# Weights fetched in order of use and cast by GpSimd, and the first block transposed on TensorE

## The chip, the cores and the metric

The kernel runs on the 8 cores of one Trainium2 chip, each core on 4 of the 32 sequences, with its own copy of the weights. No core talks to another. The metric is the device time of the slowest core in microseconds (us). Time before: 1548.24 us, the median of 3 runs (1544.91 to 1763.65).

## The reference

One layer of a streaming encoder, in float32:

```python
x = layer_norm(x, ln0_g, ln0_b)                      # entry norm, 1024 columns
proj = einsum('bsd,de->bse', x, w_in)                # w_in: 1024 x 4096
q, k, v, z_a, bg, cg, h, z_c = split(proj, 8)        # 512 columns each
# 8 heads of 64; a chunk of 64 frames sees itself and 8 chunks before it,
# with a learned relative bias
y_att  = chunk_attention(q, k, v, rel_bias) * silu(z_a)
y_conv = bg * causal_conv3(cg * h) * silu(z_c)
x = layer_norm(alpha * x + concat(y_att, y_conv) @ w_out, ln_g, ln_b)
```

The weights are 16.8 MB (`w_in`) and 4.2 MB (`w_out`) in float32; the kernel keeps both in SBUF in bf16. Each core has 4 x 2048 tokens.

## The kernel before

**Tiling.** The 8192 tokens of a core are 16 blocks of 512 tokens (`NTB`), each of 4 tiles of 128 tokens (`TPB`). A block goes through these stages: entry norm of its four tiles (`ln0_*`: statistics on DVE, four small GpSimd operations in `ln0_small`, two DVE passes over the tile in `ln0_res_a` and `ln0_res_b`, a bf16 copy `xhb` on ACT and a DMA transpose into `xnT` in `ln0_act`); `stage_P1`, 64 matmuls for q and k; `stage_attn`, eight heads, in which the score matmuls (`stage_QK`), the weighted sums of the head before (`stage_PV`) and the projections for v, z_a and the convolution (`unit_v`, `unit_za`, `unit_C`, `unit_zc`, `unit_B`, `unit_h`: 192 matmuls) are interleaved; then `stage_out`, 64 matmuls with `w_out`, and the last norm in `out_tile`. While block b is in `stage_attn`, the entry norm of block b+1 is done by DVE, GpSimd and ACT; `stage_P1(b+1)` runs before `stage_out(b)`. What `unit_h` leaves of the convolution for channel groups 2 and 3 (`late`) runs on DVE after the eight heads. Every fourth block (0, 4, 8, 12) begins a sequence and has no block before it to attend to.

**Order.** The program is written as one list per engine (`Prog`); each engine runs its list in order and waits on semaphores for what an instruction reads or overwrites. So the order in which the Python code calls `P.op` and `P.dma` is the order on each queue. All plain DMAs and DMA transposes are issued by SP (SyncE), in one queue. A GpSimd operation always waits for the one before it (`op`, line 62).

**Start of the kernel before.** SP issues the constant tables (lines 258 to 264: four 512 KB tables, three small ones, and `rtab` of 1 MB), then the four x tiles of block 0, then two weight chunks. All the tables count on one semaphore (`fix_dma_key`), so that the first DVE operation that reads any of them (line 275) waits for all. DVE scales the tables and builds `etab` (the bias, line 288) and then norms the four tiles. A weight chunk is 128 rows of `w_in` by 1024 columns, 512 KB (`wchunks`): the first eight chunks hold the columns of q and k, the next eight v and z_a, and so on. It lands in one of three staging buffers (`w_stage`: pieces of `yT`, `ytok`, later `xhb` and `xs`), and DVE casts it to bf16 (line 324). `w_item(n)` issues the DMA of chunk n+2 and casts chunk n. Chunks 0 to 15 stand ahead of `stage_attn(0)`; chunks 16 to 39 are background items (`bg`) of its heads 0, 1 and 2. The x tiles of block 1 are loaded by SP after chunk 17's DMA and, the last, after all chunks.

Of the kernel before, what the change touches and what calls it, by code (L numbers as in the profile page):

```python
# [165 lines left out]
def build(nseq, seqlen):  # L166
# [112 lines left out]
    P.op("dve", lambda e: e.tensor_scalar(out=cwh[:], in0=cwh[:], scalar1=0.5, scalar2=None, op0=ALU.mult),
         reads=["cwh"], writes=["cwh"])  # L280
    P.op("dve", lambda e: e.tensor_scalar(out=cbh[:], in0=cbh[:], scalar1=0.5, scalar2=None, op0=ALU.mult),
         reads=["cbh"], writes=["cbh"])
    P.op("dve", lambda e: e.tensor_scalar(out=nrc[:], in0=nrc[:], scalar1=-1.0, scalar2=None, op0=ALU.mult),
         reads=["nrc"], writes=["nrc"])
    rtab_sb = xs[:, 6:8, :].rearrange("p a d -> p (a d)")
    NEG = -240000.0
    for h in range(H):
        P.op("dve", lambda e, h=h: e.tensor_scalar(out=etab[:, h, :], in0=rtab_sb[:, h * 256:(h + 1) * 256],
                                                   scalar1=nrc[:, h:h + 1], scalar2=8.0, op0=ALU.add, op1=ALU.mult),
             reads=["xs6", "xs7", "nrc"], writes=["etab"])  # L290
    P.op("pool", lambda e: e.memset(etab[64:128, :, 0:64], NEG), reads=["etab"], writes=["etab"])

    yT_f = yT[:, :, :].rearrange("p a b -> p (a b)").bitcast(F32)
    ytok_f = ytok[:, :, :].rearrange("p a b -> p (a b)").bitcast(F32)
    stg = [yT_f[:, 0:1024], yT_f[:, 1024:2048], ytok_f[:, 0:1024]]
    stg_res = [["yT%d_%d" % (g, t) for g in range(2) for t in range(TPB)], ["yT%d" % c for c in range(4, 8)],
               ["ytok0", "ytok1"]]

    wchunks = []
    for g in range(4):  # L300
        for kc in range(8):
            wchunks.append((w_in_d[kc * 128:(kc + 1) * 128, g * 1024:(g + 1) * 1024],
# [515 lines left out]
```

How the kernel before makes its waits and increments, by code:

```python
        def run(e, eng):  # L112
            seen = {}
            for ins in self.q[e]:
                need = {}
                for kind, ev in ins["deps"]:
                    if self._skip(kind, ev, e):
                        continue
                    if ev[0] == "e":
                        k = ("e", ev[1])
                        v = self.q[ev[1]][ev[2]]["cnt"]
                    else:
                        k = ("d", ev[1])
                        v = ev[2]
                    if v > need.get(k, 0):
                        need[k] = v
                for k, v in need.items():
                    if seen.get(k, 0) >= v:
                        continue
                    seen[k] = v
                    eng.wait_ge(esem[k[1]] if k[0] == "e" else dsem[k[1]], v)
                    stats[e][1] += 1
                if ins["fn"] is None:
                    continue
                r = ins["fn"](eng)
                ins["name"] = r.ins.name
                if ins["dma"] is not None:
                    r.then_inc(dsem[ins["dma"][0]], 16)
                elif ins["mark"]:
                    r.then_inc(esem[e], 1)
```

## Time and profile before

| what | value |
|---|---|
| median of the runs | 1548.24 us |
| the profiled execution, its own time | 1546.93 us |
| its span, first to last instruction, slowest core (core 1) | 1545.4 us |
| spans of the eight cores | 1537.7 to 1545.4 us |
| PE / DVE / ACT / GpSimd busy | 90% / 71% / 42% / 17% of the span |
| `stage_P1(0)` matmuls | 50.4 to 80.1 us |
| `stage_attn(0)` on PE | 80.1 to 176.1 us |
| `stage_P1(1)` and `stage_out(0)` on PE | 176.1 to 203.9 us |
| `stage_out(3)` to `stage_out(4)`, start to start | 87.5 us (458.1 to 545.7) |

The span is cut into 40 slices on the page; in the first four (0 to 155 us) PE is busy 0, 4, 6 and 6 tenths, and 8 or 9 from there on. Line numbers such as L418 are those of the kernel before. "xhb<-w_in" names a transfer or an operation by what it writes and reads; so the weight DMAs appear under the names of the buffers that they are staged in.

### The profile page before, as it was taken

How to read it: one execution, taken by the hardware profiler on the slowest of the kernel's cores; microseconds unless marked ns; L12 is line 12 of the kernel's file. 1: busy time of each engine (PE TensorE's matmuls, PEld its weight loads, DVE VectorE, ACT ScalarE, POOL GpSimd, SP SyncE). 2: the span in 40 equal slices, each digit the busy share in tenths (PEclk: the TensorE clock that was granted, in tenths of full speed). 3: DMA queues.
4: the chain of work that ended last, by engine and by line, in shares of the span. 5: the costliest groups of instructions: out<-in, count | busy, mean ns of one | idle time of the engine just before them, and what ended most of it. 6: DMA issues, size and time to landing. Idle time of an engine off the chain costs nothing.

```text
span 1545.4 us, 28780 instructions; the slowest of 8 cores (1537.7 to 1545.4 us)
## 1 busy us (share of the span) xinstructions
...
## 2 busy tenths in 40 slices
...
GB/s 177 185 258 149 35 110 39 54 81 22 117 35 110 42 70 72 24 110 28 110 42 84 61 48 87 25 117 35 107 41 52 83 24 121 28 110 42 54 10 62
DMA packets 129940, 118.27 MB, mean 77 GB/s; under 512 B 107648, under 2 KB 107648, under 8 KB 129664
## 3 DMA queue, kind: packets, MB, share of 16 engines
...
q14 instruction: 73, 0.60, 0.1%
...
## 4 chain that ended last, share of the span: by engine, by line
PE 65%; DVE 17%; issue 9%; DMA 6%; ACT 2%; POOL 1%; DVEq 1%; SPq 0%; ACTq 0%; POOLq 0%
PE mm L418 27%; PE mm L699 14%; PE mm L429 13%; PE sc L573 5%; DVE stats L346 3%; DVE xs L395 3%; PE pv L607 3%; DMA xhb<-w_in 3%; PE sc L580 2%; ACT PT L586 2%; DMA yT<-w_in 2%; DVE ynorm L616 1%; DVE acc L534 1%; DVE acc L538 1%; DVE xs L387 1%
## 5 line engine op out<-in xcount | busy, mean ns | idle before, releaser
L418 PE MATMUL mm<-xnT,w_in_sb 128*128 128x512 bf16 x3072 | 780.9, 385 | 116.1 <-DMA xnT<-xhb 51.2
L586 ACT ACTIVATE PT<-sc 128x384 bf16<-128x384 f32 (+1 forms) x672 | 342.6, 526 | 409.3 <-PE sc L580 194.7
L418 PEld LDWEIGHTS mm<-xnT,w_in_sb 128*128 128x128 bf16 x3072 | 290.5, 99 | 382.1 <-issue 143.8
L429 PE MATMUL mm<-w_in_sb,xnT 128*128 128x512 bf16 x1024 | 254.8, 381 | 8.2 <-DVE gate L491 6.7
L573 PE MATMUL sc<-qz,kT 128*128 128x512 bf16 (+3 forms) x896 | 239.8, 301 | 5.4 <-ACT PT L586 3.8
L607 PEld LDWEIGHTS pv<-vA,PT 128*128 128x128 bf16 x2240 | 161.3, 99 | 161.8 <-issue 10.9
L699 PE MATMUL mm<-w_out_sb,yT 128*128 128x512 bf16 x1024 | 227.8, 383 | 5.4 <-DMA yT<-ytok 3.9
L607 PE MATMUL pv<-vA,PT 128*128 128x65 bf16 x2240 | 183.8, 194 | 3.5 <-ACT PT L586 3.5
L704 DVE TENSOR_TENSOR xs<-xs,mm 128x512 f32<-128x512 f32 x128 | 87.9, 687 | 137.2 <-PE mm L699 136.3
L699 PEld LDWEIGHTS mm<-w_out_sb,yT 128*128 128x128 bf16 x1024 | 100.8, 99 | 129.4 <-issue 11.3
L580 PE MATMUL sc<-etab,ident 128*128 128x256 bf16 (+1 forms) x608 | 155.1, 255 | 0.0
L429 PEld LDWEIGHTS mm<-w_in_sb,xnT 128*128 128x128 bf16 x1024 | 96.9, 98 | 93.5 <-issue 10.7
L717 POOL TENSOR_SCALAR rstd<-mv 128x1 f32<-128x1 f32 x64 | 26.7, 418 | 522.2 <-DVE mv L711 522.2
L573 PEld LDWEIGHTS sc<-qz,kT 128*128 128x128 bf16 x896 | 81.8, 98 | 45.4 <-issue 12.3
L708 DVE BATCH_NORM_STATS2 stats<-xs 128x6 f32<-128x512 f32 x128 | 88.9, 694 | 13.9 <-DVE xs L704 0.9
L361 POOL TENSOR_SCALAR rstd<-mv 128x1 f32<-128x1 f32 x64 | 26.4, 413 | 386.6 <-DVE rden L614 201.7
L346 DVE BATCH_NORM_STATS2 stats<-xs 128x6 f32<-128x512 f32 x128 | 88.2, 689 | 5.2
L593 POOL MEMSET PT<- 64x128 bf16 x192 | 38.0, 198 | 288.8 <-ACT PT L586 276.6
L743 DVE SCALAR_TENSOR_TENSOR xs<-xs,rstd,b1bc_sb 128x1024 f32<-128x1024 f32 x64 | 82.2, 1284 | 7.1 <-DVE xs L730 0.5
L387 DVE SCALAR_TENSOR_TENSOR xs<-xs,nmean,ag 128x1024 f32<-128x1024 f32 x64 | 81.9, 1280 | 6.9 <-POOL nmean L367 6.6
L465 ACT ACTIVATE qz<-mm 64x512 bf16<-64x512 f32 x64 | 37.8, 591 | 115.7 <-PE mm L418 115.7
L491 DVE SCALAR_TENSOR_TENSOR gate<-tz,mm 128x512 bf16<-128x512 f32 x64 | 43.9, 686 | 55.4 <-ACT tz L489 33.1
...
## 6 DMA issues: line engine op xcount, KB each, us to landing
xs<-x SPq DMA_DIRECT2D x64, 512.0 KB, 4.4
out<-xs SPq DMA_DIRECT2D x64, 512.0 KB, 5.2
yT<-w_in SPq DMA_DIRECT2D x11, 512.0 KB, 5.7
xhb<-w_in SPq DMA_DIRECT2D x11, 512.0 KB, 5.6
ytok<-w_in SPq DMA_DIRECT2D x5, 512.0 KB, 5.2
xs<-w_in SPq DMA_DIRECT2D x5, 512.0 KB, 6.4
xhb<-w_out SPq DMA_DIRECT2D x5, 512.0 KB, 4.9
yT<-ytok SPq DMA_TRANSPOSE x128, 2.3
```

Of the source, the lines that this page charges most:

```text
L346: P.op("dve", lambda e, t=t, s=s, k=k: e.bn_stats(out=stats0[:, t, k, :], in_=xs[:, s, k * 512:(k + 1) * 512]), reads=["xs%d" % s], writes ...
L387: P.op("dve", lambda e, t=t, s=s: e.scalar_tensor_tensor(out=xs[:, s, :], in0=xs[:, s, :], scalar=nmean0[:, t:t + 1], in1=ag0[:], op0=ALU. ...
L418: P.op("pe", lambda e, i=i, kc=kc, cc=cc: e.matmul(mm[i][:, :], lhsT=w_in_sb[:, kc, cc * 128:(cc + 1) * 128], rhs=xnT[:, sl, kc, :], start ...
L429: P.op("pe", lambda e, i=i, kc=kc, t=t, c0=c0: e.matmul(mm[i][:, :], lhsT=xnT[:, sl, kc, t * 128:(t + 1) * 128], rhs=w_in_sb[:, kc, c0:c0 ...
L573: sp=(len(extra) == 0): e.matmul(sc[i][:, coff:coff + n], lhsT=kT[:, ks, pair, kt * 128:(kt + 1) * 128], rhs=qz[:, pair, hh, LO[j] * 64:(H ...
L580: P.op("pe", lambda e, i=i, a0=a0, nn=nn, hq=src[1], c=src[2], last=last: e.matmul(sc[i][:, a0:a0 + nn], lhsT=ident[:], rhs=etab[:, hq, c: ...
L586: P.op("act", lambda e, i=i, coff=coff, hb=hb, j0=j0: e.activation(out=PT[:, hb, OFF[j0]:OFF[j0] + coff], in_=sc[i][:, 0:coff], func=AF.Ex ...
L607: st=(idx == 0), sp=(idx == len(items) - 1): e.matmul(pvb[:, t, 0:65], lhsT=PT[:, hb, a0:a0 + 128], rhs=vA[:, ks, j % 4, h, 0:65], start=s ...
L699: P.op("pe", lambda e, i=i, c=c, t=t, hf=hf: e.matmul(mm[i][:, :], lhsT=yT[:, c, t * 128:(t + 1) * 128], rhs=w_out_sb[:, c, hf * 512:(hf + ...
L704: P.op("dve", lambda e, i=i, s=s, hf=hf: e.tensor_tensor(out=xs[:, s, hf * 512:(hf + 1) * 512], in0=xs[:, s, hf * 512:(hf + 1) * 512], in1 ...
L708: P.op("dve", lambda e, t=t, s=s, hf=hf: e.bn_stats(out=stats1[:, t, hf, :], in_=xs[:, s, hf * 512:(hf + 1) * 512]), reads=xr, writes=["st ...
L743: P.op("dve", lambda e, t=t, s=s: e.scalar_tensor_tensor(out=xs[:, s, :], in0=xs[:, s, :], scalar=rstd1[:, t:t + 1], in1=b1bc[:], op0=ALU. ...
```

## The change

Both weights now arrive as a list (`stream`) of chunks in the order in which block 0 uses them. On the host `w_in` is re-ordered into 8 groups (g) of 512 columns, each of 4 chunks of 512 KB that hold 256 rows: g0 and g1 are q and k of two head pairs each, g2 is v, g3 z_a, and g4 to g7 hold the four column blocks (C, z_c, B, h) of one channel group each. A chunk lies in one piece in HBM. For g0 to g3 six staging buffers take turns: two x slots, the buffers of the last norm's tables (`g1bc`, `b1bc`), a new buffer `stg`, and half of `vA` that block 0 does not use; from g4 on the last four of them. `stream_pump` issues DMAs as far as buffers are free, and `cast_next` casts the next chunk on GpSimd. `need_w(g)` runs the casts up to group g; it is called in the projections of block 0 and at the start of its head h for g = 3 + h. Between the groups stand `rtab` (after g1), the two tables of the entry norm (after g3) and the x tiles of block 1 (after g4 and g5). The last norm's tables come last.

SP's first DMAs are the x tiles of block 0, and the small constants come as one piece (`cst`). Block 0 gets another entry norm: ACT writes (x - mean) * rstd to `xhb` (`ln0_xhat`), 32 TensorE transposes put it into PSUM, and ACT and DVE copy it to `xnT` with gain and bias per partition (`first_T`). The two DVE passes over the four tiles that the residual needs (`ln0_res_a`, `ln0_res_b`) move behind `stage_attn(0)`. The statistics buffers are doubled, and the small operation that wrote `nmr0` stays for block 0 only. The matmuls of all blocks are as many as before; their weight columns lie elsewhere (`wcol`).

```diff
-    w_in_d = din("w_in", [D, NCOLS])
+    w_in_d = din("w_in", [8, 4, 128, 1024])
...
-    for dst, src, nm in ((ag0, g0bc_d, "ag0"),
-                         (ab0, b0bc_d, "ab0"), (g1bc, g1bc_d, "g1bc"), (b1bc, b1bc_d, "b1bc"),
-                         (cwh, cw_d, "cwh"), (cbh, cb_d, "cbh"), (nrc, rc_d, "nrc")):
-        P.dma("sp", lambda e, dst=dst, src=src: e.dma_start(out=dst[:], in_=src), "c", writes=[nm])
...
+    for t in range(TPB):
+        load_tile(0, t)
+    P.dma("sp", lambda e: e.dma_start(out=cst[:], in_=cst_d), "cst", writes=["cst"])
...
+    early = [(xs[:, 4, :], ["xs4"]), (xs[:, 5, :], ["xs5"]), (g1bc[:], ["g1bc"]), (b1bc[:], ["b1bc"]),
+             (stg[:], ["stg"]), (vA1_f, ["v1_%d" % t for t in range(TPB)])]
+    late_bufs = early[2:]
+
+    stream = []
+    for g in range(8):
+        for k in range(4):
+            bufs = early if g < 4 else late_bufs
+            buf = bufs[(4 * g + k) % len(bufs)]
+            stream.append(("w", buf, w_in_d[g, k],
+                           w_in_sb[:, 2 * k:2 * k + 2, g * 512:(g + 1) * 512], "w_in%d_%d" % (g, k)))
+        if g == 1:
+            stream.append(("rtab",))
+        if g == 3:
+            stream.append(("tab", ag0, g0bc_d, "ag0"))
+            stream.append(("tab", ab0, b0bc_d, "ab0"))
+        if g in (4, 5):
+            for t in (0, 1):
+                stream.append(("x", 2 * (g - 4) + t))
     for kc in range(8):
...
+        stream.append(("w", late_bufs[kc % len(late_bufs)], w_out_d[kc * 128:(kc + 1) * 128, :],
+                       w_out_sb[:, kc, :], "w_out%d" % kc))
...
+    def cast_next():
+        stream_pump()
...
+            P.op("pool", lambda e: e.tensor_copy(out=dst, in_=buf), reads=res, writes=[it[4]])
+        elif it[0] == "rtab":
+            build_etab()
...
+        cast_done[0] += 1
+        stream_pump()
...
-    def w_cast(n):
-        buf, bres, key = w_stage(n)
-        dst, res = wchunks[n][1], wchunks[n][2]
-        P.op("dve", lambda e, buf=buf, dst=dst: e.tensor_copy(out=dst, in_=buf), reads=bres, writes=[res])
...
+    def first_T():
+        for kp in range(4):
+            i = next_mm()
+            for kk in range(2):
+                kc = 2 * kp + kk
+                for t in range(TPB):
+                    P.op("pe", lambda e, i=i, kc=kc, kk=kk, t=t: e.transpose(
+                        mmb[i][:, kk * 512 + t * 128: kk * 512 + (t + 1) * 128],
+                        xhb[:, t, kc * 128:(kc + 1) * 128], ident[:]),
+                        reads=["xhb%d" % t, "ident"], writes=["mm%d" % i])
...
-            if b == 0 and h < 3:
-                bg += [lambda n=n: w_item(n) for n in range(16 + 8 * h, 24 + 8 * h)]
-                if h == 2 and nxt is not None:
-                    bg.append(lambda: load_tile(1, 3))
+            if b == 0:
+                need_w(min(7, 3 + h))
...
+    stream_pump()
+    for t in range(TPB):
+        ln0_stats_k(0, t, 0)
+        ln0_stats_k(0, t, 1)
+        ln0_aggr(0, t)
+        ln0_small(0, t)
+        ln0_xhat(0, t)
+    scale_consts()
+    first_T()
     drive(stage_P1(0))
...
         late = stage_attn(b, has_prev, nxt)
         for f in late:
             f()
+        if b == 0:
+            for t in range(TPB):
+                ln0_res_a(0, t)
+                ln0_res_b(0, t)
         if nxt is not None:
             drive(stage_P1(nxt))
+        if b == 0:
+            while cast_done[0] < len(stream):
+                cast_next()
```

In the rows that follow an engine's own operations stand in its order; "[waits ...]" names the semaphores (`s_dve` is DVE's, `d_...` a DMA's). First GpSimd at the start of the program, before: behind the four small operations of each of the four tiles (the last tile's are shown) come the small operations of block 1.

```order
L291 MEMSET etab 64x8x64 [waits s_dve,s_pool]
...
L361 TENSOR_SCALAR rstd<-mv 128x1 [waits s_dve,s_pool]
L364 TENSOR_TENSOR rstd<-rstd,nhalf 128x1 [waits s_pool]
L367 TENSOR_SCALAR nmean<-mv 128x1 [waits s_pool]
L370 TENSOR_TENSOR nmr<-nmean,rstd 128x1 [waits s_pool]
```

The same place now, from the last small operation of tile 3 on: the eight casts of g0 and g1, the memset of `etab`, and the casts of g2.

```order
L404 TENSOR_TENSOR nmr<-nmean,rstd 128x1 [waits s_pool]
L364 CAST w_in_sb<-xs 128x2x512 [waits d_ws_xs4,s_pool]
L364 CAST w_in_sb<-xs 128x2x512 [waits d_ws_xs5,s_pool]
L364 CAST w_in_sb<-g1bc_sb 128x2x512 [waits d_ws_g1bc,s_pool]
L364 CAST w_in_sb<-b1bc_sb 128x2x512 [waits d_ws_b1bc,s_pool]
L364 CAST w_in_sb<-stg 128x2x512 [waits d_ws_stg,s_pool]
L364 CAST w_in_sb<-vA 128x2x512 [waits d_ws_v1_0,s_pool]
L364 CAST w_in_sb<-xs 128x2x512 [waits d_ws_xs4,s_pool]
L364 CAST w_in_sb<-xs 128x2x512 [waits d_ws_xs5,s_pool]
L291 MEMSET etab 64x8x64 [waits s_dve,s_pool]
L364 CAST w_in_sb<-g1bc_sb 128x2x512 [waits d_ws_g1bc,s_pool]
```

What moved: 40 casts that DVE did stand on GpSimd, each behind the one before it, and the memset of `etab`, which waits for `rtab`, stands between g1 and g2.

Second, SP around the end of `stage_attn(0)`, before: the last weight chunks and the last x tile, then the transposes of block 1's tiles and of the attention output, then the first stores.

```order
L319 DMA xhb<-w_out 128x1024 [waits d_wt0,s_dve]
L337 DMA xs<-x 128x1024 [waits d_wt2,s_dve]
L380 DMA_TRANSPOSE xnT<-xhb 128x8x128 [waits s_act] x2
L627 DMA_TRANSPOSE yT<-ytok 128x2x128 [waits s_dve,d_ws0]
L627 DMA_TRANSPOSE yT<-ytok 128x2x128 x3
L380 DMA_TRANSPOSE xnT<-xhb 128x8x128 [waits s_act] x2
L627 DMA_TRANSPOSE yT<-ytok 128x2x128 [waits s_dve]
L627 DMA_TRANSPOSE yT<-ytok 128x2x128 x3
```

The same place now:

```order
L340 DMA vA<-w_out 128x1024 [waits d_ws_v1_0,s_pool]
L420 DMA_TRANSPOSE xnT<-xhb 128x8x128 [waits s_act]
L697 DMA_TRANSPOSE yT<-ytok 128x2x128 [waits s_dve]
L697 DMA_TRANSPOSE yT<-ytok 128x2x128 x3
L420 DMA_TRANSPOSE xnT<-xhb 128x8x128 [waits s_act] x2
L697 DMA_TRANSPOSE yT<-ytok 128x2x128 [waits s_dve]
L697 DMA_TRANSPOSE yT<-ytok 128x2x128 x3
L340 DMA g1bc_sb<-w_out 128x1024 [waits d_ws_g1bc,s_pool]
L340 DMA b1bc_sb<-w_out 128x1024 [waits d_ws_b1bc,s_pool]
L340 DMA stg<-w_out 128x1024 [waits d_ws_stg,s_pool]
L340 DMA vA<-w_out 128x1024 [waits d_ws_v1_0,s_pool]
```

What moved: the last four chunks of `w_out` stand behind the transposes of the attention output (L697), which wait for DVE's last operation of the eight heads.

Third, DVE behind the eight heads. Before, the last operations of `late` and then at once the first additions of `stage_out(0)` (L704):

```order
L542 COPY halo<-ubuf 128x2
L544 TENSOR_TENSOR yT<-acc,tz 128x512 [waits s_dve]
L704 TENSOR_TENSOR xs<-xs,mm 128x512 [waits s_pe]
L708 BN_STATS stats<-xs 128x6 [waits s_dve]
```

Now:

```order
L612 COPY halo<-ubuf 128x2
L614 TENSOR_TENSOR yT<-acc,tz 128x512 [waits s_dve]
L428 SCALAR_TENSOR_TENSOR xs<-xs,nmean,ag 128x1024
L437 SCALAR_TENSOR_TENSOR xs<-xs,rstd,ab 128x1024 [waits s_dve]
L428 SCALAR_TENSOR_TENSOR xs<-xs,nmean,ag 128x1024
L437 SCALAR_TENSOR_TENSOR xs<-xs,rstd,ab 128x1024 [waits s_dve]
L428 SCALAR_TENSOR_TENSOR xs<-xs,nmean,ag 128x1024
L437 SCALAR_TENSOR_TENSOR xs<-xs,rstd,ab 128x1024 [waits s_dve]
L428 SCALAR_TENSOR_TENSOR xs<-xs,nmean,ag 128x1024
L437 SCALAR_TENSOR_TENSOR xs<-xs,rstd,ab 128x1024 [waits s_dve]
L772 TENSOR_TENSOR xs<-xs,mm 128x512 [waits s_pe]
```

What moved: eight passes over whole tiles, which stood at the start of the program, now stand between `late` and the first addition of `stage_out(0)` (L772).

## Rows read from the trace of the kernel before

**Rows 1.** Stretches: bounds, length, busy us of PE, PEld, DVE, ACT, POOL; clock; DMA.

```profile
80.10:176.10 96.00, 65.72 (x338) 29.59 (x337) 54.30 (x96) 25.17 (x45) 9.77 (x16) 0.82 0.58 170
...
472.00:531.80 59.80, 53.55 (x337) 27.20 (x335) 49.39 (x83) 24.56 (x44) 11.29 (x20) 0.97 0.34 94
...
10.00:20.00 10.00, 0.00 (x0) 0.00 (x0) 3.08 (x10) 0.00 (x0) 0.00 (x0) 1.00 0.97 320
```

**Rows 2.** Chain of waits, first 260 us: start, length, what the end waited for.

```profile
4.59 11.70 DMA xs<-rtab
...
76.27 10.15 DMA xhb<-w_in
...
140.89 1.30 DVE xs L387
...
176.19 13.87 PE mm L418 x64
190.06 13.81 PE mm L699 x64
```

**Rows 3.** Timeline to 170 us: start, length, operation, count [idle before <-releaser].

```profile
6.33 3.47 DVE L274 MEMSET qz<- 128x4096 bf16 x1 [0.80 <-issue]
...
21.51 1.49 DVE L346 BATCH_NORM_STATS2 stats<-xs 128x6 f32<-128x512 f32 x2
...
23.10 0.21 DVE L351 BATCH_NORM_AGGREGATE mv<-stats 128x2 f32<-128x12 f32 x1
...
45.94 1.06 ACT L377 ACTIVATE xhb<-xs 128x1024 bf16<-128x1024 f32 x1 [5.00 <-DVE xs L395]
...
50.44 1.01 PE L418 MATMUL mm<-xnT,w_in_sb 128*128 128x512 bf16 x2 [50.44 <-DMA xnT<-xhb]
...
65.67 14.56 PE L418 MATMUL mm<-xnT,w_in_sb 128*128 128x512 bf16 x57 [1.53 <-DVE w_in_sb L324]
...
69.77 0.60 ACT L474 ACTIVATE kT<-mm 128x512 bf16<-128x512 f32 x1 [2.21 <-PE mm L418]
```

**Rows 4.** Timeline of GpSimd (POOL) to 200 us.

```profile
1.06 0.20 POOL L266 MEMSET ident<- 128x128 bf16 x1 [0.38 <-POOLq L172]
1.48 0.29 POOL L267 TENSOR_SCALAR_AFFINE_SELECT ident<-ident 128x128 bf16<-128x128 bf16 x1 [0.21 <-POOL ident L266]
...
21.77 0.52 POOL L291 MEMSET etab<- 64x512 bf16 x1 [19.78 <-DVE etab L288]
23.54 0.22 POOL L361 TENSOR_SCALAR rstd<-mv 128x1 f32<-128x1 f32 x1 [1.25 <-DVE mv L351]
23.91 0.57 POOL L364 TENSOR_TENSOR rstd<-rstd,nhalf 128x1 f32<-128x1 f32 x1
...
25.02 0.19 POOL L370 TENSOR_TENSOR nmr<-nmean,rstd 128x1 f32<-128x1 f32 x1
...
141.21 1.39 POOL L364 TENSOR_TENSOR rstd<-rstd,nhalf 128x1 f32<-128x1 f32 x1
```

**Rows 5.** Timeline of SP: issue of the last four transposes of block 0.

```profile
178.19 4.93 SPq L627 DMA_TRANSPOSE yT<-ytok  x4
```

**Rows 6.** DMA issues to 170 us: count, KB each, median us from issue to landing.

```profile
xhb<-w_out SPq DMA_DIRECT2D x5, 512.0 KB, 4.9
...
ag<-g0bc SPq DMA_DIRECT2D x1, 512.0 KB, 3.7
...
b1bc_sb<-b1bc SPq DMA_DIRECT2D x1, 512.0 KB, 7.8
```

**Rows 7.** Groups by line, 0 to 200 us: busy us, mean ns, idle before, releaser.

```profile
L324 DVE CAST w_in_sb<-xhb 128x1024 bf16<-128x1024 f32 x11 | 7.6, 694 | 21.9 <-DMA xhb<-w_in 21.9
```

**Rows 8.** Groups of PE by line, 472 to 532 us (attention of block 4).

```profile
L418 PE MATMUL mm<-xnT,w_in_sb 128*128 128x512 bf16 x129 | 33.4, 389 | 6.3 <-DVE tz L512 4.9 <-DMA xnT<-xhb 0.8 <-DVE tz L519 0.6
```

**Rows 9.** Timeline of DVE in the attention of block 4.

```profile
500.35 0.55 DVE L530 TENSOR_SCALAR acc<-ubuf,cwh,cbh 128x512 f32<-128x512 f32 x1
...
502.71 0.69 DVE L544 TENSOR_TENSOR yT<-acc,tz 128x512 bf16<-128x512 f32 x1
```

More of the change, by code:

```diff
@@ L279, in build @@
[L279 to L302, printed above, removed]
-                            w_in_sb[:, kc, g * 1024:(g + 1) * 1024], "w_in%d_%d" % (g, kc)))
-    for kc in range(8):
-        wchunks.append((w_out_d[kc * 128:(kc + 1) * 128, :], w_out_sb[:, kc, :], "w_out%d" % kc))
@@ L340, in stage_load, with build_etab @@
-    def stage_load(b):
-        for t in range(TPB):
-            load_tile(b, t)
+    def build_etab():
+        rtab_sb = xs[:, 6:8, :].rearrange("p a d -> p (a d)")
+        P.op("dve", lambda e: e.tensor_scalar(out=cst[:, 32:40], in0=cst[:, 32:40], scalar1=-1.0, scalar2=None,
+                                              op0=ALU.mult), reads=["cst"], writes=["nrc"])
+        for h in range(H):
+            P.op("dve", lambda e, h=h: e.tensor_scalar(
+                out=etab[:, h, :], in0=rtab_sb[:, h * 256:(h + 1) * 256],
+                scalar1=nrc[:, h:h + 1], scalar2=8.0, op0=ALU.add, op1=ALU.mult),
+                reads=["xs6", "xs7", "nrc"], writes=["etab"])
+        P.op("pool", lambda e: e.memset(etab[64:128, :, 0:64], -240000.0), reads=["etab"], writes=["etab"])
@@ new lines, in cast_next @@
+    def cast_next():
+        stream_pump()
+        n = cast_done[0]
+        assert n < issued[0]
+        it = stream[n]
+        if it[0] == "w":
+            buf, res = it[1]
+            dst = it[3]
+            if len(dst.shape) == 3:
+                buf = buf.rearrange("p (a c) -> p a c", c=512)
+            P.op("pool", lambda e: e.tensor_copy(out=dst, in_=buf), reads=res, writes=[it[4]])
+        elif it[0] == "rtab":
+            build_etab()
+        elif it[0] == "tab" and it[3] in ("ag0", "ab0"):
+            scale_tab(it[1], it[3])
+        cast_done[0] += 1
+        stream_pump()
@@ L748, in out_tile_b @@
               "st%d" % s, reads=xr)
-    stage_load(0)
-    w_dma(0)
-    w_dma(1)
-    stage_ln0(0)
-    for n in range(8):
-        w_item(n)
-    drive(stage_P1(0))
-    for n in range(8, 16):
-        w_item(n)
-    if nblk > 1:
-        for t in range(3):
-            load_tile(1, t)
+    stream_pump()
[7 more added lines that the diff above has]
+    first_T()
+    drive(stage_P1(0))
+    while cast_done[0] <= stream.index(("rtab",)):
+        cast_next()
     for b in range(nblk):
```

238 lines of the change are left out of this document (143 added, 95 removed).

## Prediction, made before the change was run

> **What bounds the kernel now.** I read the time by stretches first. The eight heads of block 0 take 96.0 us (80.1 to 176.1), those of block 4, which has no block before it either and does the same matmuls, 59.8 us [rows 1]. PE is busy 65.7 us of the 96.0, at a mean granted clock of 0.82; in block 4 it is busy 53.5 us at 0.97. So some 36 us are lost there to something that block 4 does not have. The chain of waits in order of time names it: ahead of 176 us its longest pieces are transfers, the tables and `rtab` first (11.70 us), then weight chunks (up to 10.15 us); from 176.19 on it is PE at its matmuls [rows 2]. The timeline shows the second loss: the first matmul of all runs at 50.44 us, waits for the DMA transposes, and the stream of `stage_P1(0)` begins at 65.67, when the eighth cast is done [rows 3]. DVE casts are short, 0.69 us, behind 21.9 us of waiting for the 11 transfers of that group [rows 7]: not the cast, but the transfer in front of it is late. The change can move the point where `stage_P1(1)` begins, now 176.19 [rows 2], and what follows within `stage_out(0)`. Behind that the kernel is the same.
>
> **The start.** SP issues the x tiles where the four tables stood. The first and the fourth table landed 3.7 and 7.8 us after their issue [rows 6]; issued at 1.1 to 2.5 us, the tiles are there by 10.3. DVE is at its memsets until 9.80 anyway [rows 3]. Statistics take 1.49 + 0.21 us and a gap, 1.8 per tile [rows 3], so tile 3 is through at 17.1; GpSimd's four operations run from 23.54 to 25.21 in the trace, 1.7 us, with 0.2 ahead [rows 4]: 19.0. The copy on ACT takes 1.06 [rows 3]: 20.2. The transposes are not in the trace. A 512-column matmul takes 14.56 / 57 = 0.255 us in the first `stage_P1` [rows 3]; a quarter of that, eight times, is 0.5 us for a group below, eight whole ones 2.0 above. I take 0.9, nearer to the first since a transpose has 128 columns. Each group is copied in two pieces of 0.60 [rows 3], by ACT and DVE in turn; the fourth ends at 25.3 (at the upper bound 3.5 us later). The first group of `stage_P1(0)` ends at 25.8, and the other 56 matmuls at 0.255 take 14.3: **40.1 us instead of 80.1.**
>
> **The weights for it.** With a full queue DMA moves 320 GB/s at a share of 0.97 [rows 1]: 1.64 us per chunk of 0.524 MB. The first six chunks land behind the x tiles, from 11.9 to 20.1. GpSimd is free for casts at 19.0.
>
> What a cast costs there no row shows. A memset of 128 columns takes 0.20 us, one of 512 takes 0.52 [rows 4]: 0.83 ns per column, 0.95 us for 1024. The select, which reads and writes 128 columns, takes 0.29 against 0.19 for a one-column operation [rows 4]: 0.8 ns, 1.0 us. Below stands DVE's 0.69 [rows 7]; above, reading and writing one after the other, 2.0. I take 1.0, by the select, plus 0.15 between two: g0 is cast at 23.6. Chunks 6 and 7 are issued as casts 0 and 1 free their buffers and land some 4.9 us later [rows 6], so g1 is cast at 28, and needed at 25.8 + 24 x 0.255 = 31.9. `rtab` lands behind them at 29; `etab` costs DVE some 4 us, covered by `stage_P1(0)`, in which DVE has nothing else to do; without that cover it would be 4 us. g2 is then cast by 38, needed at 40.1. From 20.3 on 34 chunk lengths (24 weight chunks from g2 on, two of g1, four x tiles, `rtab` as two, two tables) take 34 x 1.64 = 56 us: g7 is there at 76, and heads 6 and 7 that use it begin, at 59.8 / 8 = 7.5 us a head [rows 1], after 85. DVE's statistics on block 1's first tile stand ahead of two gate operations on its queue, and PE's banks wait for those; the tile lands at 20.3 + 19 x 1.64 = 51.5, they want it at about 54. So transfers are hidden from 40 us on.
>
> *A rule against the change:* The Trainium skill ("GPSIMD Engine Reference", introduction) calls GpSimd the wrong choice for ordinary elementwise work, VectorE being about twice as fast; its section "Engine selection" excepts operations with one input. By the rule without the exception a cast would take 2 x 0.69 = 1.4 us, an estimate, and the sum below would be about 1492. No row here shows a wide read on GpSimd.
>
> **The heads of block 0.** I take block 4's 59.8 us. In it PE waits 6.3 us, most of it for DVE [rows 8]: heads 2 to 5 are short of DVE. To these the change adds casts. GpSimd and DVE get in each other's way: the power operation takes 0.57 us alone and 1.39 beside DVE's pass with two SBUF inputs, 140.89 to 142.19 [rows 2, 4]. 16 casts (g5, g6, g7, half of `w_out`) fall into heads 2 to 5. What DVE waits for a cast no row shows: nothing below, a whole cast of 1.0 above, so 0 to 16 us. I take half, 8, since some half of DVE's work there has two SBUF inputs. The heads end at E = 40.1 + 67.8 = **107.9 instead of 176.2: 68.3 us gained.** DVE's 40 casts (28 us) cost nothing now that they are gone, as it waited for transfers, and gain nothing by themselves. The scaling of two tables (1.4 us) goes under heads 0 and 1.
>
> **Behind the heads something is late.** On SP the last four `w_out` chunks stand behind the transposes of the attention output. These wait for DVE's last head operation, about E + 1.1, and their issue takes 4.93 us [rows 5]. The chunks land from E + 11 (4.9 us after issue [rows 6]) to E + 16. Meanwhile DVE does `late` (twice 500.35 to 503.40, 6.1 us [rows 9]) and then the eight moved passes of 1.3 us, from E + 7 on [rows 2]. If each cast waits for a pass (1.3 + 1.0), they end at E + 13.3, 15.6, 17.9 and 20.2. PE is through `stage_P1(1)` at E + 13.9 [rows 2] and ends the first group of `stage_out(0)` at E + 20.3 instead of E + 15.6: 4.7 us lost. DVE, freed at about E + 21.6, then finds groups coming every 1.73 us (13.81 / 8 [rows 2]) and keeps up. Bounds: 1.4 lost if the casts need not wait, 10 at 2.0 us each. The small operation dropped on GpSimd (0.19 us [rows 4]) and the memset of `vA`'s ones lie under `stage_P1(1)` or idle time: nothing.
>
> **Sum.** 68.3 - 4.7 = 63.6. Span 1545.4 - 63.6 = 1481.8; the profiled execution took 1.5 us more than its span, so **1483 us**. Its 1546.9 is 1.3 under the median of the runs, 1548.2, which changes nothing here.
>
> **Rivals.**
> 1. *DVE waits a whole cast each time*: 16 instead of 8, 1491. For it: GpSimd waited to the end of DVE's pass in [rows 4]. Against: much of DVE's work reads PSUM. The Trainium skill ("SBUF — State Buffer", section "SBUF: two separate sides") says that whichever starts first holds the pair for a whole instruction and the other blocks; on GpSimd's side the trace agrees (1.39 against 0.57 us).
> 2. *DVE does not wait at all*, and the last casts slip in: 8 + 3.3 less, 1472. For it: no DVE row is stretched beside GpSimd, but these operations were short.
> 3. *A cast takes 2.0 us.* g1 is cast at 19.0 + 8 x 2.15 = 36.2 (`stage_P1(0)` 1.5 later), g2 at 45.3 (4.5 more), g3 2.3 and g4 1.8 late: 10 us; half a cast of waiting, 16 times, is 8 more, and behind the heads 5: 1506.
> 4. *Transfers bind all the same.* From 80 to 176 us the trace moves only 170 GB/s [rows 1]: 3.1 us per chunk, g7 at 20.3 + 34 x 3.1 = 126, E at 142 after its cast and two heads of 7.5, 1517. Against it: the share was 0.58 there, three buffers did not fill the queue, and with more in flight it reached 0.97.
> 5. *Slower: GpSimd becomes the bound.* The 32nd cast ends at 19 + 32c, heads 6 and 7 take 15 us more; E reaches 171.5, where nothing is gained, at c = 4.3 us, and 2% slower at c = 5.3. The rows speak for a quarter of that; a cast with its 3-D pattern has not been seen.
>
> **How the numbers follow.** My forecast 0.42 (its own range 1477 to 1489), rival 1 0.18, rival 2 0.17, rival 3 0.12, rival 4 0.06, rival 5 0.05. The range reaches from below rival 2 (1466) to rival 3 (1509); rivals 4 and 5 and part of 3 stay outside. About 2%, 31 us, can be told from no change, so faster means below 1517: the first four and half of rival 4, 0.92; the same 0.06; slower 0.02.
>
> **What would show it.** Right: first `stage_P1` matmul before 27 us and its end near 40; weight casts on GpSimd of about 1.0 us; heads of block 0 in 60 to 76 us, with PE's waits there on DVE and not on casts or transfers; `stage_out(0)` beginning some 5 us late, on GpSimd. From `stage_P1(2)` on the blocks should keep their 87 to 90 us. Wrong: PE waiting for casts in heads 2 to 7 (rivals 3, 5), DMA share near 1 up to E (rival 4), or a slower later block, which I hold for unchanged.

## The result, and the profile after

| | median | ratio to before, 95% interval |
|---|---|---|
| before | 1547.38 us | |
| changed kernel | 1490.83 us (1480.33 to 1493.75) | 0.9622, 0.9569 to 0.9674 |
| changed kernel, measured again later | 1481.52 us | 0.9575, 0.9563 to 0.9588 |

The change makes the kernel faster by about 4%. In most executions of the first measurement two or four cores ran at a mean granted clock of 0.968 instead of 0.985 to 0.988 and took up to 1492 us, which its profiled execution (1480.33 us, span 1478.8, slowest core 5) and the repeat do not show and whose cause is open, and a few executions in which a whole die fell further (up to 1697 us here) are in the medians but not in the ratios.

The timeline of PE, core 5 (start, length, operation, count, [idle before <-releaser]), answers to [rows 2, 3]:

```profile
20.32 3.45 PE L448 MATMUL mm<-ident,xhb 128*128 128x128 bf16 x29 [1.55 <-ACT xhb L411]
23.56 14.02 PE L486 MATMUL mm<-xnT,w_in_sb 128*128 128x512 bf16 x64
...
92.10 1.44 PE L486 MATMUL mm<-xnT,w_in_sb 128*128 128x512 bf16 x3 [4.75 <-DVE tz L582]
...
103.10 13.97 PE L486 MATMUL mm<-xnT,w_in_sb 128*128 128x512 bf16 x64
116.91 1.24 PE L767 MATMUL mm<-w_out_sb,yT 128*128 128x512 bf16 x5
119.44 0.38 PE L767 MATMUL mm<-w_out_sb,yT 128*128 128x512 bf16 x1 [1.28 <-POOL w_out_sb L364]
121.51 0.38 PE L767 MATMUL mm<-w_out_sb,yT 128*128 128x512 bf16 x1 [1.70 <-POOL w_out_sb L364]
123.49 15.39 PE L767 MATMUL mm<-w_out_sb,yT 128*128 128x512 bf16 x57 [1.60 <-POOL w_out_sb L364]
```

The first `stage_P1` now runs from 23.6 to 37.4 in one piece (before: 50.4 to 80.1, in pieces). `stage_P1(1)` begins at 103.1 instead of 176.2. `stage_out(0)`, the rows with `w_out_sb`, is broken three times by casts and ends at 138.7. The stretches of the heads of block 0 and of `stage_out(0)` (columns as in [rows 1]):

```profile
37.40:103.10 65.70, 54.40 (x337) 26.66 (x336) 41.94 (x72) 24.87 (x45) 38.24 (x39) 0.97 0.89 254
...
120.00:140.00 20.00, 16.89 (x66) 7.18 (x67) 15.19 (x22) 0.54 (x2) 6.40 (x12) 0.83 0.13 45
...
123.50:129.50 6.00, 6.00 (x15) 2.16 (x16) 3.69 (x6) 0.00 (x0) 0.10 (x1) 0.50 0.00 0
```

The heads take 65.7 us instead of 96.0, at a clock of 0.97 instead of 0.82, and the DMA share there is 0.89; the fullest stretch before had 0.97 [rows 1]. In `stage_out(0)` the 6 us behind the third wait run at a granted clock of 0.50. GpSimd, SP and DVE in the same profile:

```profile
21.32 1.04 POOL L364 CAST w_in_sb<-g1bc_sb 128x1024 bf16<-128x1024 f32 x1
...
115.60 1.72 POOL L364 CAST w_out_sb<-g1bc_sb 128x1024 bf16<-128x1024 f32 x1 [21.37 <-DMA g1bc_sb<-w_out]
...
121.39 1.84 POOL L364 CAST w_out_sb<-vA 128x1024 bf16<-128x1024 f32 x1
```

```profile
105.17 4.93 SPq L697 DMA_TRANSPOSE yT<-ytok  x4
110.26 0.45 SPq L340 DMA_DIRECT2D g1bc_sb<-w_out  x1
```

```profile
58.19 0.69 DVE L384 BATCH_NORM_STATS2 stats<-xs 128x6 f32<-128x512 f32 x1 [5.20 <-DMA xs<-x]
...
116.33 2.06 DVE L428 SCALAR_TENSOR_TENSOR xs<-xs,nmean,ag 128x1024 f32<-128x1024 f32 x1
```

A cast takes 1.04 us alone and up to 1.87 (at 87.23) beside a wide DVE pass, which takes up to 2.06 instead of 1.28. The fifth `w_out` chunk is issued at 110.26, right behind the four transposes, and its cast is the one behind 21.37 us of idle time. DVE waited 5.20 us for the first x tile of block 1. Behind `stage_out(0)` little changed: from its end to the end of the span 1340.1 us, before 1341.5.

### The profile page after: what moved, and what is told of

It reads as the page before. It is cut to its first block, busy times and chain, and to the rows that moved or that the text cites. A ratio compares the mean times of both kernels' runs of the same rounds, so it can differ in the third digit from the quotient of the medians.

```text
span 1478.8 us, 28799 instructions; the slowest of 8 cores (1471.5 to 1478.8 us)
## 1 busy us (share of the span) xinstructions
PE 1382.6 (93%) x8896; PEld 705.1 (48%) x8896; DVE 1080.5 (73%) x1810; ACT 656.2 (44%) x1189; POOL 295.9 (20%) x629
## 4 chain that ended last, share of the span: by engine, by line
PE 68%; DVE 15%; issue 8%; DMA 3%; POOL 2%; ACT 2%; SPq 0%; DVEq 0%; ACTq 0%; POOLq 0%
PE mm L486 29%; PE mm L767 15%; PE mm L499 13%; PE sc L643 5%; PE pv L677 3%; DVE stats L384 3%; PE sc L650 3%; DVE xs L437 2%; ACT PT L656 2%; DVE ynorm L686 1%; POOL w_in_sb L364 1%; DMA stg<-w_in 1%; DVE acc L604 1%; DVE acc L608 1%; DVE tz L582 1%
## 5 line engine op out<-in xcount | busy, mean ns | idle before, releaser
L486 PE MATMUL mm<-xnT,w_in_sb 128*128 128x512 bf16 x3072 | 768.0, 380 | 41.2 <-DVE tz L582 33.8
L767 PE MATMUL mm<-w_out_sb,yT 128*128 128x512 bf16 x1024 | 231.0, 387 | 10.0 <-POOL w_out_sb L364 4.6
L772 DVE TENSOR_TENSOR xs<-xs,mm 128x512 f32<-128x512 f32 x128 | 87.9, 687 | 130.7 <-PE mm L767 129.9
L437 DVE SCALAR_TENSOR_TENSOR xs<-xs,rstd,ab 128x1024 f32<-128x1024 f32 x64 | 84.2, 1316 | 1.1
L428 DVE SCALAR_TENSOR_TENSOR xs<-xs,nmean,ag 128x1024 f32<-128x1024 f32 x64 | 84.2, 1315 | 0.0
```

Source lines behind the costliest of these rows:

```text
L428: P.op("dve", lambda e: e.scalar_tensor_tensor(out=xs[:, s, :], in0=xs[:, s, :], scalar=nmean0[:, u:u + 1], in1=ag0[:], op0=ALU.add, op1=A ...
L437: P.op("dve", lambda e: e.scalar_tensor_tensor(out=xs[:, s, :], in0=xs[:, s, :], scalar=rstd0[:, u:u + 1], in1=ab0[:], op0=ALU.mult, op1=A ...
L486: P.op("pe", lambda e, i=i, kc=kc: e.matmul(mm[i][:, :], lhsT=w_in_sb[:, kc, c0:c0 + 128], rhs=xnT[:, sl, kc, :], start=(kc == 0), stop=(k ...
L767: P.op("pe", lambda e, i=i, c=c, t=t, hf=hf: e.matmul(mm[i][:, :], lhsT=yT[:, c, t * 128:(t + 1) * 128], rhs=w_out_sb[:, c, hf * 512:(hf + ...
L772: P.op("dve", lambda e, i=i, s=s, hf=hf: e.tensor_tensor(out=xs[:, s, hf * 512:(hf + 1) * 512], in0=xs[:, s, hf * 512:(hf + 1) * 512], in1 ...
```

## The experiments

Each is an edit of the changed kernel; L364 is the cast in it. Where a core is not named, ranges are over the eight cores of the profiled execution; the changed kernel's heads of block 0 took 62.3 to 65.8 us there, and its `stage_out(0)` ended between 132.1 and 138.9. The runs were made on several chips, on which the kernel before took 1546 to 1549 us; differences of 2 or 3 us between two runs below are therefore at the edge of what can be told apart.

**The changed kernel again.** 

> The changed kernel itself, nothing edited, to see what separates its executions: 1480.3 where all cores show a mean clock of .985 to .988, 1490 to 1494 where a pair or two of cores show .968. If that fall belongs to the kernel, most executions here show it again and the median is 1488 to 1494; if it belongs to the chip or its state in that measurement, it is rare here and the median is 1479 to 1483.

1481.52 us: the second case of the expectation. So the prediction is to be compared with 1480 to 1482.

**Without the new start of block 0.** Block 0 is normed and transposed as before (tables first, DVE's passes, DMA transposes); only the weights come the new way.

```diff
-        ln0_xhat(0, t)
+        ln0_res_a(0, t)
+        ln0_res_b(0, t)
+        ln0_act(0, t)
...
-    first_T()
...
```

> The changed kernel with block 0 normed as before the change: the two tables first behind the x tiles, two DVE passes per tile, copy on ACT, DMA transposes on SP; weights as changed. Theory (the transposes on TensorE bring the start forward): stage_P1(0) starts near 40 us instead of 23.6, the weights from chunk 6 on are issued behind the transposes and come 15 to 18 us later, heads end 15 to 20 us later, stage_out(0) loses 2 us less since DVE has no passes behind the heads: 1493 to 1500 us where the changed kernel takes 1480. Rival (the weights bind anyway, so the earlier start is only waited away later): under 5 us slower.

1497.89 us, ratio 0.9667 (0.9623 to 0.9712). PE's first row on core 0:

```profile
42.27 16.25 PE L485 MATMUL mm<-xnT,w_in_sb 128*128 128x512 bf16 x64 [42.27 <-POOL w_in_sb L365]
```

It begins 18.7 us later than in the changed kernel, and 16.4 us of that remain at the end (1497.9 - 1481.5). So 16 of the 66 us hang on the new start of block 0, and 49 (1547.1 - 1497.9, same chip) are there without it, by the weights' part of the change as a whole: the order, the buffers and GpSimd's casts, which this run does not part.

The 16 us are not the transposes' own. ACT's copy of tile 3 to `xhb`, which the last transposes wait for, in this run (core 0) and in the changed kernel (core 5):

```profile
37.91 1.06 ACT L419 ACTIVATE xhb<-xs 128x1024 bf16<-128x1024 f32 x1 [5.59 <-DVE xs L438]
```

```profile
18.93 1.24 ACT L411 ACTIVATE xhb<-xs,nmr,rstd 128x1024 bf16<-128x1024 f32 x1 [0.58 <-POOL nmr L404]
```

It ends at 39.0 and at 20.2, and from there the first matmul is some 3.3 us away in both (42.27 and 23.56). So what comes sooner is the copy, since DVE's two passes over each tile, and the tables that they need, no longer stand ahead of it; whether the DMA would transpose in the new order just as soon was not run. (The row above names a cast as the last to end; the last DMA transpose landed at 42.1, at about the same time.) The time agreed with the theory, but the cause that it named is not shown. One more thing differs: the 64 matmuls took 16.25 us here and 14.02 in the changed kernel, which the account of the start below takes up.

**The casts on VectorE.**

```diff
-            P.op("pool", lambda e: e.tensor_copy(out=dst, in_=buf), reads=res, writes=[it[4]])
+            P.op("dve", lambda e: e.tensor_copy(out=dst, in_=buf), reads=res, writes=[it[4]])
```

> The changed kernel with its 40 casts on DVE instead of GpSimd, at the same places of the order; all else as changed. Theory (GpSimd's casts cost DVE little: in the trace of the changed kernel DVE operations beside casts are 3.6 us longer in sum over heads 2 to 5, and on DVE 16 casts of 0.69 us would cost 11): heads of block 0 longer by 7 to 15 us, stage_P1(0) later by about 4 since the first casts stand behind DVE's copies of the transposes; 1490 to 1500 us in executions in which the changed kernel takes 1480. Rival (the shared port is what costs, so taking casts off GpSimd gains): same or faster, 1470 to 1480.

1501.61 us, 0.9689 (0.9636 to 0.9741): 20 us more than with GpSimd, though a cast takes 0.69 instead of 1.04. The theory held, in the sum a little beyond its range. Heads 69.7 to 74.2 us; and in `stage_out(0)`, by the waits of PE on core 0 (total, times, longest):

```profile
PE mm L767 <- DVE w_out_sb L364: 10.8, 5, 5.6
```

In DVE's list the last casts stand behind the eight residual passes.

**The casts on ScalarE.**

```diff
-            P.op("pool", lambda e: e.tensor_copy(out=dst, in_=buf), reads=res, writes=[it[4]])
+            P.op("act", lambda e: e.activation(out=dst, in_=buf, func=AF.Copy), reads=res, writes=[it[4]])
```

> The changed kernel with its 40 casts on ScalarE instead of GpSimd, nothing else moved. Theory (an engine's own time counts less than its order: in the heads ScalarE is busy 6 to 9 us of every 20, so 20 casts of about 1.06 us fit, but the four casts of a weight group stand at the start of a head ahead of that head's exps, and each waits for its transfer, one every 1.7 us or so while the transfers are full): TensorE waits 3 to 6 us per head for scores in heads 1 to 5, heads of block 0 80 to 95 us instead of 65.6, undisturbed execution 1495 to 1510. Rival (what GpSimd's casts cost VectorE, 0.24 us each by the casts alone in block 4, is saved, and ScalarE has the room): heads 60 to 63 us and 1475 to 1479.

1498.40 us, 0.9689 (0.9672 to 0.9706); a cast took 1.05 us. The sum was right, the place was not: the heads took 66.3 to 70.6 us, not 80 to 95. On core 0 the time went into the first `stage_P1`, which lasted to 46.4 (casts and the copies of its results share ScalarE's list), and into `stage_out(0)`:

```profile
PE mm L767 <- ACT w_out_sb L364: 9.8, 8, 3.1
PE sc L643 <- ACT PT L656: 4.2, 2, 2.8
PE mm L486 <- ACT w_in_sb L364: 3.8, 3, 1.8
```

On an engine with other work in order, each cast waits for that, and that for each cast.

**The casts by themselves.** 32 more casts in the heads of block 4, which have no transfers of weights.

```diff
+            if b == 4:
+                for k in range(4):
+                    P.op("pool", lambda e: e.tensor_copy(out=stg[:].bitcast(BF16)[:, 0:1024], in_=ag0[:]),
+                         reads=["ag0"], writes=["stg"])
```

> The changed kernel with 32 more GpSimd casts in the heads of block 4 (four at the start of each head, fp32 128x1024 of a table into a staging buffer that nobody reads; no transfer goes with them): the price of the casts by themselves. Block 4's heads have no weights to wait for. Theory (a cast costs VectorE about 0.23 us in the mean by stretching the passes beside it, 3.6 us over block 0's casts): VectorE's passes in those heads grow by 5 to 10 us in sum, and the heads of block 4 by 2 to 8 us. Rival 1 (the port costs nothing that ends on the path): heads of block 4 within 1 us of the changed kernel's. Rival 2 (the price of the prediction, half a cast for each, or more): 14 us or more.

Heads of block 4 on core 5, the changed kernel first, then with the casts (columns as in [rows 1]):

```profile
406.80:467.20 60.40, 54.78 (x338) 27.57 (x337) 48.82 (x82) 24.90 (x44) 10.19 (x16) 0.94 0.33 92
```

```profile
405.70:469.70 64.00, 54.85 (x338) 27.20 (x337) 56.35 (x82) 24.46 (x44) 53.63 (x48) 0.95 0.32 87
```

DVE is busy 7.5 us longer at the same 82 operations, 0.24 us a cast. The heads took 57.7 to 60.4 us on the eight cores before and 64.0 to 65.4 with the casts, 5.3 us more in the mean: **0.16 us of the path for each cast.** The casts gave way too: the 32 took 1.38 us in the mean, 1.04 at the least. The price holds whatever a cast delays, the small GpSimd operations behind it in the list included; the run does not part these from DVE's stretched passes. Which operations grow, by line (count | busy us, mean ns | idle before):

```profile
L690 DVE TENSOR_TENSOR ytok<-ynorm,gate 128x256 bf16<-128x256 f32 x7 | 3.0, 426 | 1.3 <-DVE ynorm L686 0.8
...
L428 DVE SCALAR_TENSOR_TENSOR xs<-xs,nmean,ag 128x1024 f32<-128x1024 f32 x4 | 5.1, 1279 | 0.0
...
L582 DVE SCALAR_TENSOR_TENSOR tz<-tz,mm 128x512 f32<-128x512 f32 x4 | 2.7, 685 | 3.2 <-ACT tz L580 3.2
...
L612 DVE COPY halo<-ubuf 128x2 f32<-128x2 f32 x2 | 0.3, 160 | 0.0
```

```profile
L428 DVE SCALAR_TENSOR_TENSOR xs<-xs,nmean,ag 128x1024 f32<-128x1024 f32 x4 | 6.3, 1576 | 0.0
...
L690 DVE TENSOR_TENSOR ytok<-ynorm,gate 128x256 bf16<-128x256 f32 x7 | 4.3, 612 | 1.3 <-DVE ynorm L686 0.8
...
L582 DVE SCALAR_TENSOR_TENSOR tz<-tz,mm 128x512 f32<-128x512 f32 x4 | 2.7, 681 | 1.1 <-ACT tz L580 1.1
...
L612 DVE COPY halo<-ubuf 128x2 f32<-128x2 f32 x2 | 2.0, 1002 | 0.0
```

L428 and L690, with two inputs in SBUF, grow (1.28 to 1.58, 0.43 to 0.61), L582, with one input in PSUM, does not (0.685 and 0.681), and the copy of two columns, L612, takes 1.00 us instead of 0.16. The Trainium skill ("SBUF — State Buffer", section "Who interferes with whom") names these kinds: VectorE instructions with two SBUF inputs contend with GpSimd instructions that read SBUF for a shared port pair, and so can copies, in a mode that uses both pairs. The trace agrees for these four rows; in which mode the copy ran no row shows. Not every operation with two SBUF inputs grew: L604 stayed at 0.75 us and L614 at 0.69 and 0.68.

**Three staging buffers.**

```diff
-    late_bufs = early[2:]
+    early = early[2:5]
+    late_bufs = early
```

> The changed kernel with three staging buffers throughout instead of six and four. Theory of the prediction (transfers are hidden from 40 us on, weights are ahead by a head or more): heads of block 0 end at most 3 us later. Rival (transfers do bind in the heads: in the trace of the changed kernel the DMA share is 0.8 to 1.0 from 48 to 94 us, PE waits 2.2 us for casts and DVE 5.2 us for an x tile): three buffers move some 262 GB/s as in the kernel before, 2.0 us per chunk instead of 1.64, and the heads end 8 to 15 us later, 1488 to 1495 us where the changed kernel takes 1480.

1497.25 us, 0.9660 (0.9616 to 0.9705): 16 us later, where hidden transfers would have allowed 3. PE's waits on core 5:

```profile
PE mm L487 <- POOL w_in_sb L365: 7.7, 7, 2.8
...
PE mm L500 <- POOL w_in_sb L365: 4.2, 4, 1.4
```

The heads took 71.0 to 78.9 us, with 227 GB/s in those of core 5, and up to 5 us are lost ahead of them (they begin at 39.6 to 43.5 instead of 37.4 to 38.6). The rival held, and was still too small: how many transfers are under way decides when PE gets its weights, so they are not hidden.

**x tiles ahead.** x(1,0) is fetched ahead of group 4 and x(1,1) behind it, then the two tables, then group 5.

```diff
         if g == 3:
+            stream.append(("x", 0))
+        if g == 4:
+            stream.append(("x", 1))
             stream.append(("tab", ag0, g0bc_d, "ag0"))
...
```

> The stream's order alone is changed: x(1,0) ahead of weight group 4, x(1,1) right behind it, and the two tables of LN0 behind that. Theory (the heads of block 0 are held by transfers: VectorE waited 5.2 us for the first x tile, its passes came late, and TensorE then waited 4.75 us for tz at 92 us and ran three more microseconds at a lower granted clock behind that wait): VectorE's wait for x falls to under 1.5 us, TensorE's wait for tz to under 2 us, the heads take 58 to 62 us instead of 65.6, undisturbed execution 1473 to 1477. Rival (the transfers are full and only the order of the lateness changes): TensorE waits 3 us or more for group 4 or the res passes wait for the tables, heads again 64 to 67 us, 1479 to 1484.

1482.31 us, 0.9575 (0.9558 to 0.9591), heads 63.1 to 65.9: as before. DVE's waits in the heads of core 4, and PE's:

```profile
DVE ag L298 <- DMA ag<-g0bc: 2.5, 1, 2.5
DVE ab L298 <- DMA ab<-b0bc: 0.6, 1, 0.6
```

```profile
PE mm L491 <- DVE tz L587: 4.7, 1, 4.7
PE mm L491 <- POOL w_in_sb L369: 4.5, 5, 1.5
```

The wait of 5.2 us for x is gone; 3.1 us for the tables and 4.5 for casts took its place. The theory fell in its second half too: PE's 4.7 us for `tz` is not the late x tile's doing. Block 4 waits for `tz` as well: 4.9 us in two waits before [rows 8], 4.8 in the changed kernel.

**`w_out` earlier, two places.** First at the start of head 6:

```diff
                 if h == 6:
+                    while cast_done[0] <= w_pos[35]:
+                        cast_next()
```

> The changed kernel with the DMAs of the last four w_out chunks issued at head 6, ahead of the transposes of the attention output on SP; nothing else moved. Theory (these chunks are late because they stand behind those transposes): the three waits of PE for casts in stage_out(0), 4.6 us, and the lower clock behind them, 3 us more for 57 matmuls, both go: 6 to 8 us faster than the changed kernel in like executions. Rival (the eight moved DVE passes hold stage_out(0) just as long): PE then waits for DVE at the fourth group, gain under 2 us.

The median was 1504.38 us (0.9664), the fastest execution 1483.95. On core 0, SP and then PE:

```profile
94.86 1.25 SPq L420 DMA_TRANSPOSE xnT<-xhb  x1
96.28 0.46 SPq L340 DMA_DIRECT2D g1bc_sb<-w_out  x1
...
98.28 2.51 SPq L420 DMA_TRANSPOSE xnT<-xhb  x1
```

```profile
107.28 15.46 PE L486 MATMUL mm<-xnT,w_in_sb 128*128 128x512 bf16 x64 [6.09 <-DMA xnT<-xhb]
122.57 13.98 PE L770 MATMUL mm<-w_out_sb,yT 128*128 128x512 bf16 x64
```

`stage_out(0)` is whole, 13.98 us, but `stage_P1(1)` now waits 6.09 us for the last transpose, which stands behind the four loads. The stall only moved.

Measured again beside the changed kernel's repeat: 

> The kernel with w_out 4 to 7 issued at the start of head 6, unchanged, on the same chip as the changed kernel's repeat. Three of its four executions had shown pairs of cores at a mean clock of .965 to .968. If the fall comes with this kernel, it shows again (1500 or more); if it comes with the chip, it is 1482 to 1486 here whenever the changed kernel's repeat shows none.

1483.66 us, 0.9587 (0.9569 to 0.9605), the second case of the expectation; the changed kernel has 0.9575. So the early loads gain nothing, and `stage_P1(1)` waits 5.4 to 8.2 us on every core.

Then at the end of head 6, behind the last transpose of block 1's tokens and ahead of those into `yT`:

```diff
                 ln0_act(nxt, h - 3)
+                if b == 0 and h == 6:
+                    while cast_done[0] <= w_pos[35]:
+                        cast_next()
```

> w_out 4 to 7 are issued on SP after the last transpose of block 1's tokens (end of head 6) and ahead of the eight transposes into yT's second half; nothing else moves. Theory (stage_out(0) of the changed kernel lost 4.6 us to casts that came late because their transfers stood behind the yT transposes on SP, and another 3.1 us because the matmuls ran at a lower granted clock behind those waits): casts of w_out 4 to 7 done by about 113, stage_out(0) unbroken in about 14 us on every core, slowest undisturbed core 1471 to 1474 us against 1478.8, so an undisturbed execution of 1473 to 1477; P1(1) waits for no transpose more than before. Rival (the transposes give the stall back, as with the loads at the start of head 6): stage_out or P1(1) waits 4 us or more elsewhere and the undisturbed execution stays at 1480. Whether pairs of cores fall to the clock of 0.81 is not settled by this change; the median goes with them.

1479.11 us, 0.9555 (0.9539 to 0.9572), against 0.9575 for the changed kernel. SP and PE on core 0:

```profile
95.56 5.18 SPq L420 DMA_TRANSPOSE xnT<-xhb  x2
100.89 0.47 SPq L340 DMA_DIRECT2D g1bc_sb<-w_out  x1
...
104.79 5.50 SPq L697 DMA_TRANSPOSE yT<-ytok  x4
```

```profile
116.53 5.34 PE L770 MATMUL mm<-w_out_sb,yT 128*128 128x512 bf16 x24
124.51 8.79 PE L770 MATMUL mm<-w_out_sb,yT 128*128 128x512 bf16 x40 [2.64 <-DVE xs L775]
```

No wait for a cast is left. Five cores wait some 2.5 us for DVE instead and three have no wait, but `stage_P1(1)` waits some 2.2 us for its transposes there. `stage_out(0)` ends at 132.3 to 137.1. Of the 7.7 us named in the theory (4.6 + 3.1), 2.4 arrived, and the two intervals overlap.

**Both edits.** 

> The two edits together. If both losses are real and apart, they add: undisturbed execution 1466 to 1472 us, heads 58 to 62 us and stage_out(0) unbroken. If the transfers alone bind, the gain is that of the better one, 1473 to 1478.

1478.36 us, 0.9552 (0.9533 to 0.9570): with the last version the fastest, and not told apart from it. The two do not add; the gain is that of the better one.

**Residual passes later, on top of both.** Those of tiles 2 and 3 of block 0 go behind the first two tiles of `stage_out(0)`.

```diff
             ln1_small(t)
+            if b == 0 and t < 2:
+                ln0_res_a(0, t + 2)
+                ln0_res_b(0, t + 2)
...
```

> The version with both edits (w_out 4 to 7 issued behind the last transpose of block 1's tokens, x tiles ahead of the tables), and besides the residual passes of block 0's tiles 2 and 3 recorded behind the first and the second tile of stage_out(0) instead of ahead of it. With both edits stage_out(0) still waited 0.8 to 2.6 us on VectorE, whose eight residual passes of 1.28 us end after the first matmul groups. Theory: that wait goes, stage_out(0) takes 14.0 us on every core, and the execution is 1475 to 1478. Rival: the same passes then hold the adds of stage_out(0) and block 1's first heads, and the time is 1477 to 1480 as before.

1475.61 to 1482.17 us, ratio 0.9562 (0.9546 to 0.9579). Seven of eight cores wait exactly 2.29 us in `stage_out(0)`, the eighth 2.51: the passes stand in front of other adds now. The rival held.

## Why the prediction came out as it did

The prediction was 1483 us, made from a profiled execution and to be held against one: 1480.33, in the repeat 1481.39 (median 1481.52). The median first measured, 1490.83, is outside the forecast's own range (1477 to 1489) and inside the whole one. Its steps on core 5:

| step | predicted | measured |
|---|---|---|
| `stage_P1(0)` ends | 40.1 | 37.4 |
| a cast on GpSimd | 1.0 | 1.04 |
| heads of block 0 | 67.8 | 65.7 |
| `stage_P1(1)` begins (E) | 107.9 | 103.1 |
| lost in `stage_out(0)` | 4.7 | 7.8 |
| gain of the span | 63.6 | 66.6 |

*The start* was right up to the first group. Eight transposes take 3.45 / 29 x 8 = 0.95 us (taken: 0.9), and tile 3's copy ends at 20.2 (20.2). The first matmul does not wait for the last copy from PSUM: it needs one piece of 128 rows and runs at 23.56, so that the first group ends at 25.3 for 25.8. The other 2.2 us lie in the 56 matmuls behind it, 12.1 us where the prediction took 14.3: it used 0.255 us each, the mean of a row [rows 3] whose first eleven matmuls were slow. The kernel before, in two pieces of that row:

```profile
65.67:69.94 4.27, 4.26 (x11) 1.51 (x12) 1.39 (x2) 1.35 (x3) 0.00 (x0) 1.00 0.87 283
69.94:80.10 10.16, 10.16 (x49) 4.62 (x48) 3.28 (x5) 5.17 (x9) 0.00 (x0) 1.00 0.82 229
```

That is 0.39 us each, then 0.21. The eleven began 0.43 us apart, as the matmuls of `stage_out(0)` do at a granted clock of 0.50; the clock column has 1.00 there, so that it was the clock is a reading and not shown. In the changed kernel TensorE does its 32 transposes just ahead and all 64 matmuls take 0.219 (14.02 / 64); without these transposes the 64 took 16.25 us again.

*The price of the casts* was right in kind and too high in size. The prediction gave 16 casts in heads 2 to 5 half a cast each, 8 us. By the casts alone a cast costs 0.16 us of the path; 20 casts begin between 51.9 us and the end of the heads, so 3.3 us by this estimate. PE's waits say nearly the same. In the heads of block 0 (core 5):

```profile
PE mm L486 <- DVE tz L582: 6.4, 2, 4.7
PE mm L486 <- POOL w_in_sb L364: 2.2, 2, 1.3
PE mm L499 <- POOL w_in_sb L364: 1.0, 3, 0.4
PE mm L486 <- DVE tz L589: 0.9, 1, 0.9
PE mm L486 <- DVE gate L561: 0.8, 1, 0.8
```

In the heads of block 4, same core and kernel:

```profile
PE mm L486 <- DVE tz L582: 4.8, 2, 3.3
PE mm L486 <- DVE tz L589: 0.7, 1, 0.7
```

PE waits 8.1 us for DVE where block 4 has 5.5: 2.6 us more, the late x tile included. The prediction was right that some half of DVE's work there has two SBUF inputs (28 of 48.8 us in block 4). Its half a cast was too much, since the cast waits in part itself (1.38 us for 1.04) and some of DVE's 0.24 us per cast does not end on the path. Rival 1 (a whole cast each) falls by the same run, and rival 2 (none) too.

*"So transfers are hidden from 40 us on"* failed, and what it cost took up part of that surplus: by the same waits 3.2 us for casts, which the prediction had at nothing. It moved 34 chunks at 1.64 us each and had g7 there at 76; SP issued g7's last chunk at 77.88, when a cast had freed its buffer, and its cast began at 83.8. x(1,0) was reckoned at 51.5; DVE got it at 58.2. The pace of [rows 1] is that of a full queue, and with four buffers, each waiting for its cast, the queue held it only in part: 254 GB/s in the mean of the heads. Of the 3.2 us, g4 cost 0.96 and g5 1.26; in the latter the port has its part, since the group's last two casts took 1.74 and 1.84 us. The other 1.0 (0.31, 0.31, 0.36) are those of g2, which stand behind the memset of `etab`, and that behind `rtab`, there at 31.9 for 29. Together 3.2 + 2.6 = 5.8 us of waits above block 4's, where the heads are 5.3 longer (65.7 - 60.4; PE is busy 0.4 less). Rival 4 was thus half true in its cause, and far off in its price. With three buffers it costs 16 us; changing the order only changes who waits.

*Behind the heads* the place, the cause and the engine were right: `w_out` 4 to 7 behind the transposes on SP, casts and passes in turn, 4.6 us of waits (1.28 + 1.70 + 1.60) for 4.7. What the term lacked is the clock. The 57 matmuls behind the waits took 0.270 us each (15.39 / 57), in `stage_P1(1)` 0.218 (13.97 / 64): 3 us more, with 6 us at a granted clock of 0.50. The trace of before held such a stretch: PE waiting, and a clock of 0.82 in the mean [rows 1]. It is not so on every core: on cores 4 and 7, with 1.8 and 1.6 us of waits in all, the matmuls behind them took 0.22 us each.

So the forecast of the sum was helped by luck: two terms ahead of E were too long, by 2.7 and 2.1 us, one behind it was 3.1 too short, and the rest of the span, held for unchanged, gave 1.4 (1340.1 for 1341.5 us). 63.6 + 4.8 - 3.1 + 1.4 is the measured 66.6 to within 0.1.

**What stays open.** What the order of the weights is worth by itself: no run takes it away alone, with the buffers and GpSimd's casts kept. Nor does a run part TensorE's transposes from DVE's passes, which the new start moved together. How the 0.16 us divide between the port and GpSimd's own list. And the 4.7 us wait for `tz` at 92 us, the longest left in the heads: no run removed it.
